# Block inverses of a chunked delta rule: the first turn of each block, and the turn behind the first merge, moved from TensorE to VectorE

## The reference, cut to what matters

```python
def gdn_chunked(q, k, v, g, beta, s0):
    ...
    lmat = jnp.where(strict, jnp.einsum('bnhcd,bnhed->bnhce', kb, k) * decay, 0.0)
    a = lmat + jnp.eye(C, dtype=jnp.float32)
    rhs = jnp.concatenate([vb, kb * jnp.exp(g)[..., None]], axis=-1)
    sol = lax.linalg.triangular_solve(a, rhs, left_side=True, lower=True, unit_diagonal=True)
    u, w = sol[..., :V], sol[..., V:]
    ...
    S, o = lax.scan(step, s0, xs)
```

## Time and profile before

| quantity | value |
|---|---|
| median of 3 runs | 1157.89 us (1156.71 to 1159.18) |
| time of the profiled execution | 1158.06 us |
| its span, first to last instruction | 1156.0 us |
| mean granted TensorE clock | 0.988 |
| PE busy | 1105.9 us (96%) |
| DVE busy | 493.5 us (43%) |
| ACT busy | 320.5 us (28%) |

### The profile page before, as it was taken

One profiled execution on the slowest core, in us unless ns is written; L12 is line 12 of the kernel. 1 busy time (PEld: TensorE's weight loads), 2 busy tenths in 40 slices (PEclk: granted clock), 3 DMA queues, 4 the chain that ended last, 5 costly groups with the idle time before them and its releaser, 6 DMA issues.

```text
span 1156.0 us, 13585 instructions
## 1 busy us (share of the span) xinstructions
PE 1105.9 (96%) x5452; PEld 764.0 (66%) x5452; DVE 493.5 (43%) x1120; ACT 320.5 (28%) x785; POOL 121.8 (11%) x167
## 2 busy tenths in 40 slices
PE   5997999999999999999998899999999999999997
PEld 2434555456465566796898788688875665566786
DVE  5532312851825457948558700700009326454004
ACT  1273121100112235531220111611151256544112
POOL 4000000010100022110022300700000110010001
PEclk9998999997999999999999999999999999999999
DMA  8732444120023220000031212532122200000002
GB/s 267 264 110 73 146 136 158 34 72 1 1 73 89 67 73 1 17 22 1 1 107 40 92 37 74 190 121 64 37 73 73 71 15 1 1 1 1 11 27 92
DMA packets 68406, 79.00 MB, mean 68 GB/s; under 512 B 2684, under 2 KB 63479, under 8 KB 68344
## 3 DMA queue, kind: packets, MB, share of 16 engines
q1 hardware_dynamic: 64114, 69.36, 18.7%
q0 software_dynamic: 2560, 8.05, 2.0%
q10 hardware_dynamic: 1669, 0.72, 0.2%
HBM read 74.62 MB, written 3.51 MB: 68 GB/s over the span
## 4 chain that ended last, share of the span: by engine, by line
PE 85%; DVE 8%; ACT 4%; issue 1%; POOL 1%; DMA 1%; ACTq 0%; POOLq 0%; DVEq 0%
PE ps L1195 78%; PE ps L1350 4%; PE ps L1225 2%; DVE xreg L2158 1%; DVE phase L2166 1%; ACT hT L884 1%; DVE xreg L2180 1%; ACT phase L1165 1%; PE ps L1235 0%; DVE xreg L1901 0%; DVE pad L2082 0%; DMA wring<-in_mod_w 0%; DVE pad L2089 0%; POOL stat L638 0%; DVE phase L2303 0%
## 5 line engine op out<-in xcount | busy, mean ns | idle before, releaser
L1195 PE MATMUL ps<-hT,wring 128*128 128x512 f32 (+2 forms) x1376 | 364.9, 425 | 4.3 <-ACT hT L884 4.3
L1195 PEld LDWEIGHTS ps<-hT,wring 128*128 128x128 f32 x1376 | 205.1, 192 | 157.9 <-issue 153.3
L1195 PE MATMUL ps<-phase 128*128 128x512 f32 (+4 forms) x522 | 167.9, 466 | 11.0 <-DMA phase<-k_pos_p 4.0
L1195 PE MATMUL ps<-wring,mix 128*128 128x256 f32 x640 | 140.3, 382 | 3.5 <-issue 2.7
L1195 PEld LDWEIGHTS ps<-phase 128*128 128x128 f32 (+2 forms) x522 | 86.7, 193 | 78.3 <-issue 63.8
L1195 PEld LDWEIGHTS ps<-wring,mix 128*128 128x128 f32 x640 | 122.6, 192 | 20.8 <-issue 2.9
L1195 PE MATMUL ps<-wring,hT 128*128 128x256 f32 (+1 forms) x480 | 99.5, 370 | 0.0
L1195 PEld LDWEIGHTS ps<-wring,hT 128*128 128x128 f32 x480 | 89.0, 190 | 10.3
L2206 DVE SCALAR_TENSOR_TENSOR phase<-phase,yst 128x1024 f32<-128x1024 f32 x10 | 12.8, 1284 | 124.6 <-POOL yst L638 124.6
L1195 PE MATMUL ps<-xreg,phase 128*128 128x128 f32 (+1 forms) x420 | 55.7, 292 | 7.5 <-DVE xreg L2172 4.9
L1195 PE MATMUL ps<-hT,phase 128*128 128x64 f32 (+3 forms) x258 | 59.6, 367 | 0.0
(11 more groups left out here) (310 smaller groups left out, 1214.9 us busy)
## 6 DMA issues: line engine op xcount, KB each, us to landing
wring<-in_mod_w SPq DMA_DIRECT2D x24, 1024.0 KB, 5.1
wring<-in_even_in_w SPq DMA_DIRECT2D x16, 1024.0 KB, 6.8
wring<-in_odd_in_w SPq DMA_DIRECT2D x9, 1024.0 KB, 5.8
wring<-in_even_out_w SPq DMA_DIRECT2D x4, 1024.0 KB, 7.4
wring<-in_odd_out_w SPq DMA_DIRECT2D x4, 1024.0 KB, 5.3
xreg<-in_x_sample SPq DMA_DIRECT2D x1, 2048.0 KB, 14.2
xreg<-in_x_sample POOLq DMA_DIRECT2D x1, 2048.0 KB, 8.1
out_y_sample<-xreg SPq DMA_DIRECT2D x4, 512.0 KB, 2.6
```

The lines of the kernel that those rows point to most:

```text
L1195: return nc.tensor.matmul(o, l, r, start=first, stop=last)
```

## The change: two of the four kinds of turn go to DVE

Two of the turns concern matrices that have nonzero elements only in blocks of 16x16 or 32x32 on the diagonal: the first one (U to T, ahead of the first level) and pass C of the first level (T to U, blocks of 32 by then). DVE's transpose instruction turns every 32x32 block of its operand in place, which for such a matrix is the whole transpose. In the changed kernel:

- the first turn by PE and ACT's copy of it go; DVE writes `Tinv` from `Uinv` with `transpose`, chain by chain behind each mask multiplication, and counts `T1_ready`, for which pass A of the first level waits;
- pass C of the first level and ACT's copies of it go; DVE writes `Uinv` from `Tinv` behind each addition of that level, and counts `U2_ready`, for which pass B of the second level waits;
- DVE waits in group 1, ahead of the mask multiplications, until the projection `in_z0` has been computed, because its transposes write over `hT`;
- 20 fills fall out of the ring, so that bank numbers behind them move by four (modulo eight).

```diff
-         ("inv0", CHAINS[0]), ("inv0_0", 3 * CHAINS[0]), ("keys2", 2), ("inv0_1", 3 * CHAINS[0]), ("keys3", 2),
+         ("inv0_0", 2 * CHAINS[0]), ("keys2", 2), ("inv0_1", 3 * CHAINS[0]), ("keys3", 2),
...
-         ("inv1", CHAINS[1]), ("inv1_0", 3 * CHAINS[1]), ("inv1_1", 3 * CHAINS[1]), ("inv1_2", 3 * CHAINS[1]),
+         ("inv1_0", 2 * CHAINS[1]), ("inv1_1", 3 * CHAINS[1]), ("inv1_2", 3 * CHAINS[1]),
...
@@ ScalarE @@
-                for m, (t, d) in enumerate(chains):
-                    f = g["T1"] + m
-                    wait_full(act, f)
-                    nc.scalar.activation(Tinv[t][:, d, :], bank(f), ACT.Copy).then_inc(free(f), 1)
-                for l in range(len(LEVELS)):
+                for l in range(1, len(LEVELS)):
...
@@ TensorE @@
-                keep_busy(g["T1"], 5 if g is inv_groups[1] else 3)
-                for n, (t, d) in enumerate(chains):
-                    pe.wait_ge(U1_ready, 2 * t + d + 1)
-                    turn4(g["T1"] + n, lambda h: Uinv[:, 2 * t + d, h * P:h * P + P])
+                keep_busy(g["levels"][0], 5 if g is inv_groups[1] else 3)
...
-                        wait_drained(pe, g["T1"] + n if l == 0 else g["levels"][l - 1] + nch + n)
+                        if l == 0:
+                            pe.wait_ge(T1_ready, 2 * t + d + 1)
+                        else:
+                            wait_drained(pe, g["levels"][l - 1] + nch + n)
...
-                        if l > 0:
+                        if l == 1:
+                            pe.wait_ge(U2_ready, 2 * t + d + 1)
+                        elif l > 1:
                             wait_drained(pe, g["levels"][l - 1] + 2 * nch + n)
...
-                    for n, (t, d) in enumerate(chains):
+                    for n, (t, d) in enumerate(chains if l > 0 else ()):
                         wait_drained(pe, fl + nch + n)
                         turn4(fl + 2 * nch + n, lambda h: Tinv[t][:, d, h * P:h * P + P])
...
@@ VectorE, invert_blocks @@
                 dve.wait_ge(dve_step, done[1])
+                if n == 1:
+                    wait_full(dve, start["in_z0"] + 2)
...
                            .broadcast_to([P, H, P // BASE, BASE]), ALU.mult).then_inc(U1_ready, 1)
+                        dve.wait_ge(U1_ready, 2 * t + d + 1)
+                        nc.vector.transpose(Tinv[t][:, d, :], Uinv[:, 2 * t + d, :]).then_inc(T1_ready, 1)
...
@@ VectorE, merge_level @@
                         .then_inc(free(f), 1)
+                    if l == 0:
+                        wait_drained(dve, f)
+                        nc.vector.transpose(Uinv[:, 2 * t + d, :], Tinv[t][:, d, :]).then_inc(U2_ready, 1)
```

More of the change, by code:

```diff
@@ L137, in inverse_fills @@
     for n, tiles in enumerate(GROUPS):
-        groups.append({"tiles": tiles, "chains": [(t, d) for t in tiles for d in range(2)], "T1": start[f"inv{n}"],
-                       "levels": [start[f"inv{n}_{l}"] for l in range(len(LEVELS))]})
+        groups.append({"tiles": tiles, "chains": [(t, d) for t in tiles for d in range(2)], "levels": [start[f"inv{n}_{l}"] for l in range(len(LEVELS))]})
     return groups, sums, keys
@@ L422, in program @@
         U1_ready = sem("U1_ready")
+        T1_ready = sem("T1_ready")
+        U2_ready = sem("U2_ready")
         kd_ready = sem("kd_ready")
```

## The result

| | kernel before | changed kernel |
|---|---|---|
| median | 1157.3 us (4 runs, 1155.61 to 1159.18) | 1169.21 us (4 runs, 1168.73 to 1171.01) |
| ratio, 95% interval | | 1.0105 (1.0086 to 1.0125) |
| span of the profiled execution | 1156.0 us | 1166.9 us |
| mean granted clock | 0.988 | 0.972 (0.971 or 0.972 in each of the four runs) |

What follows compares the result with a forecast made beforehand. PE, busy 96% of the span, was taken as the bound, with DVE the bound ahead of group 1's first turn. Gains of 1.75 + 1.25 + 0.5 + 2.6 = 6.1 us gave 1151.8 us, range 1149.5 to 1155.0.

Steps and rivals of the forecast that it cites:

- Group 1, first turn: Ahead of group 1's first level: PE runs behind DVE, so only 0.5 us of the turn's 3.50 us comes out.
- the rival on the other side: From group 1's pass A: clock falls and stays low, 9 us lost against 6 won, 1161 us; chance 0.04.
- the sum: Both turns in both groups: 1.75 + 1.25 + 0.5 + 2.6 = 6.1 us gained.
- the clock's two rivals: In group 1, clock falls briefly (1153.8 us, chance 0.13) or falls and stays low (1161 us, chance 0.04).
- 33 us of 64-column passes: Group 0 before: 33 us of passes, mostly 64 columns, ran at 1.00; cited against the clock staying low.
- Price of a transpose: One 128x512 transpose on DVE: 0.70 us, and 0.61 us to the start of the next independent instruction.
- the bounds of 0.48 and 1.18: DVE transpose price limits: as cheap as a copy, 0.48 us (chance 0.05), or four shuffles, 1.18 us (chance 0.12).
- Group 0: First turn gains 1.75 us, turn of the first level 1.25 us net; together 3.0 us.
- The new wait ahead of pass B of the second level: Group 0: DVE's additions for that pass come 0.70 us late, less 0.21 us of slack: 0.5 us of wait.
- The turn of the first level: Group 1: PE's turn from 567.13 to 569.76 goes to DVE with nothing late, a gain of 2.63 us.
- the prediction's contrast of 2.7 us, which brought the clock down, and 1.42 us, which did not: Earlier trace: clock fell after 2.7 us without matmuls at 660.8, not after 1.42 us ahead of group 1.

Runs made afterwards that it cites:

- run 2: Changed kernel with DVE turns only in group 0; group 1 is that of the kernel before. 1156.03 us, ratio 0.9981.
- run 5: Changed kernel with seven keep-busy products ahead of group 1, not five, and a 256-column product ahead of each pass A wait from the second chain: 1151.36 us, ratio 0.9949.
- run 8: Changed kernel with the first turn of group 1 back on PE and ACT, the other three turns on DVE: 1152.78 us, ratio 0.9955.
- run 3: Changed kernel with the first turn back on PE in both groups; DVE makes only the turn of the first level: 1153.86 us, ratio 0.9963.
- run 1: Changed kernel with seven keep-busy products ahead of group 1 in place of five, gaps inside pass A left: 1168.41 us, ratio 1.0091.
- run 9: Changed kernel with 256-column fillers inside pass A of group 1, but only five keep-busy products ahead of it: 1173.29 us, ratio 1.0135.
- run 7: Changed kernel with pass A of group 1 held until the sixth transpose, fifteen keep-busy products ahead in place of five: 1156.47 us, ratio 0.9988.
- run 4: Kernel before with four keep-busy products ahead of group 1 in place of five, all turns on PE: 1158.02 us, ratio 1.0.
- run 6: Changed kernel with four 512-column keep-busy products between the first level's pass B and the second's pass A in group 1: 1164.11 us, ratio 1.0059.
- run 10: Changed kernel with seven keep-busy products ahead of group 1 and 128-column fillers in its pass A: 1150.93 us, median of three executions, ratio 0.9939.

## Why the prediction was wrong

The step that failed is the silent one in **Group 1, first turn**, and with it the chance of 0.04 for the rival on the other side. The step priced PE's new waits there, 2.2 us ahead of pass A and 0.44 us in each chain, as waiting time alone, and the sum took every matmul at 2.4 GHz. The runs showed that these waits halve the clock for the 44 us behind them, which cost 19.0 us where the sum has nothing. The text named the right mechanism, its place and the pattern (down at pass A, held down by 64-column passes), and set the clock's two rivals together at 0.17 because 33 us of 64-column passes ran at 1.00 in the earlier trace rows. Those passes had no gaps, had transposes or key products between them, and began with the clock up. They said nothing of passes with a third of their time idle, nor of passes that begin with it down.

- **Price of a transpose:** 0.70 us taken, 0.711 us measured in all twenty, 0.64 to the next start. Right; the bounds of 0.48 and 1.18 were needlessly far.
- **Group 0:** forecast 1.75 + 1.25 = 3.0, measured 3.1 in the changed kernel and in run 2. The new wait ahead of pass B of the second level is there (509.94, in place of following pass A at 509.59), of 0.3 to 0.4 us against the 0.5 of the text. One thing was missed without harm: two mask multiplications took 1.26 and 1.01 us (last section).
- **Group 1, timing at full clock:** pass B begins where the text said: in run 5 pass B begins 14.2 us behind the start of the keep-busy products (558.83 - 544.63), where the earlier trace rows has 14.68; forecast 0.5 earlier, measured 0.5. The turn of the first level gave its 2.6 (run 8 and run 3). The whole sum is 6.1, and run 5 measured 6.1 in the trace. So the sum was right for a kernel that holds its clock, and the changed kernel does not.
- **The rival on the other side:** it priced 17 / 2 = 9 us against 6 won, and gave 1161. Its price of a record at half clock, 0.21 us, is right for 64 columns too (36.00 us for 169 records in run 1). The low stretch was longer, 44 us, for it began with pass A and ended only in the turn of the second level: 551.63 to 611.68 is 60.05 us, against 41.03 us (551.26 to 592.29) in run 5, a loss of 19.0 us. 19.0 - 6.1 is 12.9, which is what the trace of the changed kernel lost.

**What started it.** In the changed kernel it was the idle time: run 9 keeps the 2.16 us without a matmul ahead of pass A, leaves no gap behind it, and falls at the same place; in the changed kernel itself the clock was down 0.04 us after pass A had begun. With that idle time taken away, gaps of 0.44 us in every 1.32 us of a 64-column pass brought it down a little later (run 1). Run 5 differs from run 1 by the fillers alone, and the clock stays; it stays in run 7 too, with pass A held back and dense. Both were present in the changed kernel, and both had to go.

What is not settled is why 2.29 us of idle time did not bring it down in the trace of run 4, while 2.16 or 2.17 us did in the changed kernel and in runs 6 and 9, in all four executions of each by their mean clocks. The length of the idle time alone does not decide. The traces have a place that shows it: all eleven kernels traced at full speed (run 10 is not) have the same 2.68 or 2.69 us without a matmul ahead of the same 256-column products, the place of the earlier trace rows at 660.8. Behind it the clock fell in the profiled executions of the kernel before and of runs 2, 3, 4, 5, 8 and 9, and did not fall in those of the changed kernel and of runs 1, 6 and 7. The changed kernel, in the idle time and behind it:

```profile
673.10:675.80 2.70, 0.07 (x1) 0.00 (x0) 2.65 (x5) 0.00 (x0) 0.00 (x0) 1.00 0.00 0
675.90:682.00 6.10, 6.10 (x29) 5.38 (x30) 0.00 (x0) 0.38 (x1) 0.00 (x0) 1.00 0.01 3
```

What differs between these executions no trace shows. So the prediction's contrast of 2.7 us, which brought the clock down, and 1.42 us, which did not, rested on one execution of each.

**What kept it.** Shown by run 6: four wide products end the low stretch, and what then follows is again the 64-column work that had not ended it. In the kernel before, PE's own transposes stood between the passes; the change took two of PE's turns out of this stretch, the first one and that of the first level, so that 41 us went by until the next one (592.64). The turns that looked like pure cost were also what would have brought the clock back soonest. That a fall in the kernel before would have been cut short in that way is argued from this, not shown.

The Trainium skill (TensorE: Matmul & The Clock Gate, Part 4: PE-mode transpose) says that transposes don't count as work for the gate in the way that other matmuls do, so that full clock doesn't engage for them. This case's trace disagrees for 32-bit transposes: from 592.64 to 596.0 PE made only transposes, and the clock came back at the end of that stretch, after 41 us of 64-column passes had not raised it.

## What to carry to other kernels

Before a matmul pass is tied to a slower engine chain by chain, compare its work with that engine's pace, and price the difference twice: as waiting time, and as a cause for the clock to halve for what follows, here until wide products or PE's transposes came. Where a pass of narrow matmuls gets gaps, fill them (half of each gap was enough here) and the idle time ahead of it too; filling only one of the two gained nothing (run 1) or made it worse (run 9). The best kernels here are runs 10, 5 and 8 (ratios 0.9939, 0.9949 and 0.9955), whose intervals overlap; run 8 gets nearly all of the gain by leaving on PE the one turn that DVE could not make in time.

## What the runs showed of the hardware that was not expected

- What the granted clock does under the same work depends on where it stood before: dense 64-column passes held 1.00 for 21 us (run 3) and sat at 0.50 for as long as they went on (41 us in the changed kernel, 20 us in run 6, until transposes or wide products came).
- A product of 256 columns for every eight matmuls of 64 columns did not raise it (run 9, some 13 us of it).
- The same 2.68 or 2.69 us without a matmul, ahead of the same products, was followed by a fall of the clock in seven of eleven traces, and by none in the other four.
- DVE's 128x512 transpose in 32-bit floats takes 0.711 us, from and into either array.
- DVE's mask multiplication, two arrays from SBUF, stretched from 0.65 to 1.26 and 1.01 us when it met a multiplication on POOL, and the transposes between them did not. The timelines of DVE and POOL in group 0 of the changed kernel:

```profile
493.69 1.26 DVE L2095 TENSOR_TENSOR phase<-pad,phase 128x512 f32<-128x512 f32 x1
494.99 0.71 DVE L2100 STREAM_TRANSPOSE phase<-phase 128x512 f32<-128x512 f32 x1
495.62 1.01 DVE L2095 TENSOR_TENSOR phase<-pad,phase 128x512 f32<-128x512 f32 x1
```

```profile
493.13 1.28 POOL L674 TENSOR_TENSOR phase<-xreg,masks 128x512 f32<-128x512 f32 x1 [15.83 <-ACT xreg L963]
494.82 1.27 POOL L674 TENSOR_TENSOR phase<-xreg,masks 128x512 f32<-128x512 f32 x1 [0.41 <-ACT xreg L963]
496.03 2.22 POOL L677 MEMSET phase<- 128x2560 f32 x1
```

Both multiplications end 0.54 us after POOL's (494.95 and 494.41; 496.63 and 496.09), so they waited for it, and POOL's memset held nothing up. The Trainium skill (SBUF — State Buffer, SBUF: two separate sides) says that VectorE with two SBUF inputs and a GpSimd operation that reads SBUF hold a shared pair of ports one after the other, for a whole instruction; the trace agrees. It cost nothing here: the fourth transpose ended at 497.38, and pass A, which began at 497.14, reached the fourth chain some 2.6 us after its start.
